# Two of four groups of both output projections token-stationary and turned through DRAM, another order for the third group, and the first down projection's sums turned off TensorE

## What is computed

```python
def short_conv_mixer(xn, w_in, conv_w, w_out):
    gb, gc, h = jnp.split(xn @ w_in, 3, axis=-1)
    return (gb * causal_dwconv(gc * h, conv_w)) @ w_out

def conv_glu_ffn(xn, w_up, conv_w, w_down):
    gate, val = jnp.split(causal_dwconv(xn @ w_up, conv_w), 2, axis=-1)
    return (jax.nn.silu(gate) * val) @ w_down

for i in range(2):
    xn = rms_norm(h, norm_mix[i])
    mix = hgrn2_mixer(xn, ...) if i == 0 else short_conv_mixer(xn, ...)
    h = h + mix
    h = h + conv_glu_ffn(rms_norm(h, norm_ffn[i]), w_up[i], conv_w[i], w_down[i])
return rms_norm(h, final_norm)
```

## Time and profile before

| | before |
|---|---|
| median of 3 runs | 2299.27 us (2299.03 to 2299.79) |
| the profiled execution | 2299.77 us, span 2297.9 us |
| TensorE / weight loads busy | 2285.5 us (99%) / 1916.0 us (83%) |
| VectorE / ScalarE busy | 1694.5 us (74%) / 1049.6 us (46%) |
| TensorE's granted clock, mean | 0.999 |
| `HGRN_OUT` on TensorE | 405.5 to 497.8 us |
| `DOWN0` | 977 to 1222.6 us |
| `SC_OUT` | 1482.6 to 1571.7 us |

### The profile page before, as it was taken

How to read it: one execution, slowest core, us unless ns; L and a number is a source line. 1 busy time by engine, 2 the same in 40 slices (tenths; PEclk the granted TensorE clock), 3 DMA queues, 4 the chain that set the end, 5 groups by cost and what they waited for, 6 DMA issues and landing times.

```text
span 2297.9 us, 33410 instructions
## 1 busy us (share of the span) xinstructions
PE 2285.5 (99%) x11110; PEld 1916.0 (83%) x11110; DVE 1694.5 (74%) x2132; ACT 1049.6 (46%) x1089; POOL 2.8 (0%) x9
## 2 busy tenths in 40 slices
PE   9999999999999999999999999999999999999998
PEld 8888888888888888888888888888888888888887
DVE  7979788877878888865556676766878878876544
ACT  7444444454444454444444333444444444444443
POOL 0000000000000000000000000000000000000000
PEclk9999999999999999999999999999999999999999
DMA  7555555558888888875667888666888888887664
GB/s 247 166 174 160 179 164 166 183 189 236 242 245 233 244 243 240 242 214 188 191 191 208 243 238 245 202 193 197 248 242 240 242 244 236 241 249 219 220 192 155
DMA packets 389733, 493.55 MB, mean 215 GB/s; under 512 B 18704, under 2 KB 223888, under 8 KB 389520
## 3 DMA queue, kind: packets, MB, share of 16 engines
q1 hardware_dynamic: 388640, 490.01, 71.9%
q10 hardware_dynamic: 1008, 2.43, 0.3%
HBM read 459.85 MB, written 30.41 MB: 213 GB/s over the span
## 4 chain that ended last, share of the span: by engine, by line
PE 89%; DVE 6%; issue 3%; DMA 1%; ACT 1%; DVEq 0%; SPq 0%; ACTq 0%
PE acc L1459 24%; PE acc L1458 24%; PE acc L1460 24%; PE acc L1392 11%; PE acc L1402 6%; DVE w_parts L742 1%; DVE a_diag L1062 1%; DVE fpre L1047 1%; DMA raw<-in_hgrn_w_in 1%; DVE kl L1029 1%; PE side L1563 0%; DVE ql L1023 0%; ACT w_parts L463 0%; DVE ta L778 0%; DVE ta L769 0%
## 5 line engine op out<-in xcount | busy, mean ns | idle before, releaser
L742 DVE TENSOR_TENSOR w_parts<-raw,w_parts 128x1024 fp32r<-128x1024 f32 x816 | 992.8, 1224 | 551.8 <-ACT w_parts L463 425.6
L463 ACT ACTIVATE w_parts<-raw 128x1024 fp32r<-128x1024 f32 x815 | 860.1, 1059 | 1061.0 <-PE acc L1460 827.7
L1458 PE MATMUL acc<-w_parts,xn 128*128 128x512 f32 x1728 | 673.3, 390 | 0.0
L1460 PE MATMUL acc<-w_parts,xn 128*128 128x512 f32 x1728 | 672.6, 389 | 0.0
L1459 PE MATMUL acc<-w_parts,xn 128*128 128x512 f32 x1728 | 672.6, 389 | 0.0
L1458 PEld LDWEIGHTS acc<-w_parts,xn 128*128 128x128 f32 x1728 | 324.4, 188 | 67.5
L1460 PEld LDWEIGHTS acc<-w_parts,xn 128*128 128x128 f32 x1728 | 324.4, 188 | 67.2
L1459 PEld LDWEIGHTS acc<-w_parts,xn 128*128 128x128 f32 x1728 | 324.4, 188 | 66.9
L1458 PE MATMUL acc<-w_parts,act 128*128 128x512 f32 x704 | 274.3, 390 | 0.0
L1460 PE MATMUL acc<-w_parts,act 128*128 128x512 f32 x704 | 274.0, 389 | 0.0
L1459 PE MATMUL acc<-w_parts,act 128*128 128x512 f32 x704 | 274.0, 389 | 0.0
(11 more groups left out here) (157 smaller groups left out, 1223.0 us busy)
## 6 DMA issues: line engine op xcount, KB each, us to landing
raw<-in_ffn_w_up SPq DMA_DIRECT2D x352, 512.0 KB, 4.4
raw<-in_ffn_w_down SPq DMA_DIRECT2D x176, 512.0 KB, 4.6
raw<-in_hgrn_w_in SPq DMA_DIRECT2D x127, 512.0 KB, 3.8
raw<-in_sc_w_in SPq DMA_DIRECT2D x96, 512.0 KB, 4.6
crossing<-turned SPq DMA_DIRECT2D x54, 512.0 KB, 3.8
moved<-crossing SPq DMA_DIRECT2D x216, 128.0 KB, 4.5
raw<-in_hgrn_w_out SPq DMA_DIRECT2D x32, 512.0 KB, 4.0
raw<-in_sc_w_out SPq DMA_DIRECT2D x32, 512.0 KB, 4.7
```

What stands on the lines that cost most here:

```text
L463: nc.scalar.activation(w_parts[:, c % RING, :, 0, :], raw[:, c % RING], ACT.Copy).then_inc(hi_ready, 1)
L742: v.tensor_tensor(w_parts[:, c % RING, :, 1, :], raw[:, c % RING], w_parts[:, c % RING, :, 0, :].bitcast(F32), ALU.subtract).then_inc(lo_r ...
L1458: mm(bank, x_hi, hi, start=begin and q == 0, stop=False)
L1460: high = mm(bank, x_lo, hi, start=False, stop=end and q == KC - 1)
```

## The change

`HGRN_OUT` and `SC_OUT` become phases of one iteration with two groups, token-stationary; new phases `HGRN_LAST` and `SC_OUT_LAST` hold groups three and four, feature-stationary as before. In the first two groups VectorE turns the sums at the last step, SyncE stores and fetches them, and VectorE adds them to `h` at step 4 of the next group (`ADDED_AT`; HGRN scales them first), ScalarE does its `residual` at step 5 and VectorE `normed` at step 6 (`behind`). The third group's order of chunks is new: part 0 at 0, 1, 2, 6 and part 1 at 3, 4, 5, 7; all its positions are in runs of two. For the first three groups of `DOWN0` VectorE's transposes (into `turned_sums`, in the memory of `pad`) and the way through DRAM (to `moved_sums`, in that of `tb`) take the place of ScalarE's copies and TensorE's turning; the fourth group keeps them.

```diff
-        elif first and g == 0 and self is HGRN_OUT:
-            order = [(0, 0), (0, 1), (1, 0), (1, 1), (0, 2), (1, 2), (0, 3), (1, 3)]
+        elif first and g == 0 and (self is HGRN_LAST or self is SC_OUT_LAST):
+            order = [(0, 0), (0, 1), (0, 2), (1, 0), (1, 1), (1, 2), (0, 3), (1, 3)]
         elif first and g == 0 and self is HGRN_IN:
             order = [(0, 0), (1, 0), (0, 1), (1, 1), (0, 2), (0, 3), (1, 2), (1, 3)]
...
-        paired = 0 if single else self.cpg - RUN if self is HGRN_OUT and first and g == 0 else end
+        paired = 0 if single else end
         return [range(k, k + RUN) for k in range(0, paired, RUN)] + [range(k, k + 1) for k in range(paired, end)]
...
 PAIR_SPLIT, OWN_PRODUCT, OWN_HIGH, OWN_LOW = 1, 9, 10, 12
 HGRN_IN = Phase(None, 4, 4, DT, scales=3, wide_group=V_GROUP)
-HGRN_OUT = Phase(HGRN_IN, 2, 2, DT)
-UP0 = Phase(HGRN_OUT, 11, 2, DT, scales=2, corrects=False, parts=1)
+HGRN_OUT = Phase(HGRN_IN, 1, 2, DT, scales=2, corrects=False, parts=1)
+HGRN_LAST = Phase(HGRN_OUT, 1, 2, DT)
+UP0 = Phase(HGRN_LAST, 11, 2, DT, scales=2, corrects=False, parts=1)
 DOWN0 = Phase(UP0, 2, 2, FT, corrects=False, parts=1)
 SC_IN = Phase(DOWN0, 1, 10, DT, scales=10, corrects=False, parts=1)
 SC_LAST = Phase(SC_IN, 1, 2, DT, scales=2)
-SC_OUT = Phase(SC_LAST, 2, 2, DT, corrects=False)
-UP1 = Phase(SC_OUT, 11, 2, DT, scales=2, corrects=False, parts=1)
+SC_OUT = Phase(SC_LAST, 1, 2, DT, corrects=False, parts=1)
+SC_OUT_LAST = Phase(SC_OUT, 1, 2, DT, corrects=False)
+UP1 = Phase(SC_OUT_LAST, 11, 2, DT, scales=2, corrects=False, parts=1)
 DOWN1 = Phase(UP1, 2, 2, FT, corrects=False, parts=1)
 CHUNKS = DOWN1.c0 + DOWN1.n * DOWN1.cpi
 
...
+ADDED_AT, SQUARED_AT, NORMED_AT = 4, 5, 6
 SCALED_AT, CONV_AT, PRODUCT_AT, SPLIT_HIGH_AT, SPLIT_LOW_AT = 5, 6, 9, 10, 11
 
...
 
-        turned_groups = {UP0: 0, SC_IN: UP0.n * UP0.groups, UP1: UP0.n * UP0.groups + SC_IN.groups}
+        turned_groups, groups = {}, 0
+        for phase in (HGRN_OUT, UP0, DOWN0, SC_IN, SC_OUT, UP1):
+            turned_groups[phase] = groups
+            groups += phase.n * phase.groups - (phase is DOWN0)
+        stored_groups = {phase: n - (DT // TG - 1) * (n > turned_groups[DOWN0]) for phase, n in turned_groups.items()}
+
+        turned_sums = pad[:, :, TAPS - 1:].rearrange("p q (b n) -> p q b n", b=T // P)
+        moved_sums = tb[:].rearrange("p j t -> p (j t)").rearrange("p (b a n) -> p b a n", b=T // P, a=4)
 
         block = ctx.enter_context(nc.Block())
 
...
+
+            def fetch(to):
+
                 for q in range(4):
-                    sp.dma_start(moved[q * QUARTER:(q + 1) * QUARTER].rearrange("f b a n -> f (b a) n"),
+                    sp.dma_start(to[q * QUARTER:(q + 1) * QUARTER].rearrange("f b a n -> f (b a) n"),
                                  crossing[q].rearrange("b (a f) n -> f (b a) n", f=QUARTER)).then_inc(moved_in, 16)
+
+            def cross_sums(n, kk):
+
+                if n and kk == STORED_AT:
+                    sp.wait_ge(turned_ready, turned_groups[DOWN0] + n)
+                    for b in range(T // P):
+                        sp.dma_start(crossing[:, b].rearrange("q p n -> p q n"), turned_sums[:, :, b]) \
+                            .then_inc(sums_stored, 16)
+                if n and kk == FETCHED_AT:
+                    sp.wait_ge(sums_stored, 16 * (T // P) * n)
+                    fetch(moved_sums)
 
             def cross(i, first, g, kk, up):
...
 
-            def cross_conv(g, kk):
-
-                if kk == STORED_AT and 0 < g <= SC_IN.groups:
-                    store_turned(0, SC_IN, g - 1)
-                if kk == FETCHED_AT - SC_IN.cpg and g > 1:
-                    fetch_moved(0, SC_IN, g - 2)
+            def cross_next(phase, g, kk):
+
+                if kk == STORED_AT and 0 < g <= phase.groups:
+                    store_turned(0, phase, g - 1)
+                if kk == FETCHED_AT - phase.cpg and 1 < g <= phase.groups + 1:
+                    fetch_moved(0, phase, g - 2)
+
+            def cross_down(i, first, g, kk):
+
+                if first:
+                    cross_last(UP0.n - 1, g * DOWN0.cpg + kk, UP0)
+                cross_sums(i * DOWN0.groups + g, kk)
 
             def stream(phase, w, column, ahead=None):
...
-            def residual_phase(phase, r0, weight, rs_n=None, carry=None):
+            def residual_phase(phase, last, r0, weight, rs_n=None, carry=None):
+
+                def behind(g, step):
+                    if g >= 0 and step == SQUARED_AT:
+                        for part in range(TG // TW):
+                            residual(0, r0 + g * (TG // TW), part, g * TG, weight)
+
                 def pieces(i, first, g, kk):
-                    if carry and first:
+                    if carry:
                         carry(g, kk)
-                    if rs_n is not None and first and (g, kk) == (0, RS_AT):
+                    if rs_n is not None and (g, kk) == (0, RS_AT):
                         root(rs_n)
-                    part, _, _, ends = phase.steps(first, g)[kk]
-                    tile = i * (2 * TG) + g * TG
-                    if rs_n is not None and kk == phase.cpg - 1:
-                        for part in range(phase.parts):
-                            residual(i, r0 + g * phase.parts, part, tile, weight)
...
+                if (n, kk) != (DT // TG - 1, DOWN0.cpg - 1):
                     return
                 act_e.wait_ge(lo_used, DOWN0.c0 + (n + 1) * DOWN0.cpg + RING)
-                if n:
-                    act_e.wait_ge(stage_done, S_DOWN + n)
                 for b in range(T // P):
                     o = nc.scalar.activation(sums[:, b], acc[:, (DOWN0.a0 + n) % SETS, b, :], ACT.Copy)
                 o.then_inc(acc_free, 1)
...
@@ -831,47 +876,83 @@
                 low_parts(tile + part * TW, weight, TW)
                 add_squares(i, 4, sq + part, sq + part, ta[:, part * TW:(part + 1) * TW, :])
 
-            def residual_phase(phase, r0, sq0, weight, rs_n=None, rs_stage=None, ahead=None):
+            def add_moved(phase, g, tile, src):
+
+                dve.wait_ge(moved_in, (turned_groups[phase] + g + 1) * 4 * 16)
+                dst = h[:, tile:tile + TG, :].rearrange("p j (s t) -> p s j t", t=QUARTER)
+                v.tensor_tensor(dst, dst, src.rearrange("p b a (j t) -> p (b a) j t", j=TG), ALU.add).then_inc(h_ready, 2)
+
+            def residual_phase(phase, last, r0, sq0, weight, rs_n=None, rs_stage=None, ahead=None):
                 carry = carried.pop() if carried else None
 
+                def behind(g, step):
+                    if g < 0:
+                        return
+                    tile, r, sq = g * TG, r0 + g * (TG // TW), sq0 + g * (TG // TW)
+                    if step == ADDED_AT and rs_n is not None:
+                        u = pad[:, :, TAPS - 1:]
+                        scaled_moved(0, phase, g, u)
+                        await_scaled(0, phase, g)
+                        for part in range(TG // TW):
+                            dst = h[:, tile + part * TW:tile + (part + 1) * TW, :]
+                            v.tensor_tensor(dst, dst, u[:, part * TW:(part + 1) * TW, :], ALU.add).then_inc(h_ready, 1)
+                    elif step == ADDED_AT:
+                        add_moved(phase, g, tile, moved[:])
+                    if step == NORMED_AT:
+                        dve.wait_ge(h_ready, r + TG // TW)
+                        for part in range(TG // TW):
+                            normed(0, phase, r, sq, part, tile, weight)
+
+                def turns(i, first, g, kk):
+                    if ahead:
+                        ahead(i, first, g, kk)
+                    if kk == phase.cpg - 1:
+                        turn_group(i, phase, g, turned[:])
+
                 def pieces(i, first, g, kk):
-                    if carry and first:
+                    if carry and not g:
                         carry(g, kk)
-                    if rs_n is not None and first and (g, kk) == (0, FOLD_OUT_AT):
+                    if rs_n is not None and (g, kk) == (0, FOLD_OUT_AT):
                         fold_squares(rs_n)
-                    if rs_n is not None and first and (g, kk) == (0, RS_AT):
+                    if rs_n is not None and (g, kk) == (0, RS_AT):
                         rms(rs_n, rs_stage)
-                    part, _, _, ends = phase.steps(first, g)[kk]
-                    tile = i * (2 * TG) + g * TG
-                    r, sq = (n0 + g * phase.parts for n0 in (r0, sq0))
-                    if rs_n is not None and kk == phase.cpg - 1:
-                        await_corrected(i, phase, g)
+                    behind(g - 1, kk)
+
+                def last_pieces(i, first, g, kk):
+                    if g == 0:
+                        behind(phase.groups - 1, kk)
+                    part, _, _, ends = last.steps(first, g)[kk]
+                    tile = (phase.groups + g) * TG
```

(55 more changed lines are left out.)

64 lines of the change are left out of this document (40 added, 24 removed).

## The result

The changed kernel takes 2308.2 us at the median (2307.5 to 2310.3, six runs) against 2299.2 before (2299.0 to 2299.8): ratio 1.0039, 95% interval 1.0030 to 1.0049, 9.0 us slower. The forecast was 2302.4, range 2299.8 to 2306.0. The profiled execution took 2307.5 us, the fastest of the six, its span 2305.6 (before 2297.9).

A forecast was written before the change was run, and what follows sets the result against it. TensorE, busy for 99% of the span, was taken to bound the kernel. Terms -2.0 - 2.7 + 2.5 + 5.3 = +3.1 us moved the median from 2299.27 to 2302.4; range 2299.8 to 2306.0.

The forecast's parts named there:

- part 3: Seven more groups' transfers through DRAM: cost nothing, fetched sums needed 13.6 us after the transposes, there after 11.2, 2.4 cover.
- the clock: Rival, chance 0.28: TensorE's clock falls to half in the 5.3 us stall only, costing 0 to 2.1 us; 2304.5.
- Part 1: Output projections: 32 chunks go token-stationary, 2.72 us each instead of 2.78, taking 2.0 us off.
- Part 2: First down projection: three of four turn stages on TensorE go, 0.89 us each, taking 2.7 us off.
- Part 4: Between third and fourth group, TensorE waits for position 6's acc set: 2.5 us in HGRN, 5.3 in short convolution.
- The rival of the late transfer: Chance 0.08: the DRAM detour lands 2 us after its cover in both output projections, stalls 4.5 and 7.3; 2306.4.
- No new stall: Rival, chance 0.12: TensorE doesn't wait between third and fourth group, leaving -4.7 us; 2294.6.
- shorter stalls: Rival, chance 0.10: ScalarE's squares don't delay VectorE's split of position 6, stalls 1.1 and 4.7 us; 2300.4.

The follow-up runs named there:

- the part alone: Kernel before, with only the first down projection's first three groups turned by VectorE and sent through DRAM: 2296.4 us, ratio 0.9986.
- parts one after the other: Changed kernel, third group of both output projections with part 0 at positions 0 to 3, part 1 at 4 to 7: 2297.8 us, ratio 0.9995.
- the runs of one: Changed kernel, last two positions of the third group run singly (highs 6, lows 6, highs 7, lows 7): 2307.3 us, ratio 1.0036.
- the moved steps: Kernel with parts one after the other, third group's scaling, adds, squares and norm steps moved to position 1 of the fourth: 2294.3 us, ratio 0.9978.
- the part-filled second wait: Changed kernel, 8 and 18 extra matmuls of ones ahead of TensorE's two waits before the fourth group: 2306.5 us, ratio 1.0028.
- the load first: Changed kernel, SyncE issuing the fourth group's position 1 weight load ahead of the second group's fetch: 2310.5 us, ratio 1.0045.
- the release first: Changed kernel, VectorE in the short convolution's third group releasing the acc set before the second group's norm steps: 2305.0 us, ratio 1.0024.

## Why the prediction was wrong

The two waits stand where the prediction put them and end on the instructions that it named, and the form and the down projection gave what it said. Two of its terms stood at nothing and weren't: the transfers (part 3) and the clock. The sum had the right sign (+3.1), but two thirds of the size were missing: of these 5.9 us the low clock is 3.5 and the late transfers are 1.9, which leaves 0.5 open. By its steps:

- **Part 1, form, -2.0:** right (2.1 between two kernels).
- **Part 2, down projection, -2.7:** right (3.1 for the part alone, which 2.7 agrees with within the interval).
- **Part 3, the detour "a cost of nothing, with 2.4 us of cover":** wrong, the smaller of the two terms that failed, 0.7 + 1.2 = 1.9 us of wait. I took the landing times of the page, medians over the whole kernel, 3.8 and 4.5 us for store and fetch, and gave the loads behind them no term at all. Here are the issues of the stretch itself (KB each, median us to landing):

```profile
raw<-in_hgrn_w_out SPq DMA_DIRECT2D x4, 512.0 KB, 7.5
...
moved<-crossing SPq DMA_DIRECT2D x4, 128.0 KB, 5.8
```

VectorE stands for 4 us in norm steps and transposes at the second group's end and then makes three splits in a row. SyncE's queue waits 3.6 us for the transposes, and then the store, four loads and the four fetches go out between 456.97 and 465: a load needs 7.5 us at the median, a fetch 5.8, and the last fetch, on which VectorE waits, some 7.6. So the sums are there 13.6 us after the transposes began and not 11.2, and the cover of 2.4 us is used up. The trace of before had a sign of it: in the nine microseconds around the detour of the earlier trace rows four loads took 6.2 us and the fetches 5.0. Why the loads were slower still here isn't shown. Both ends of it are on the chain: VectorE waits for the fetched sums, and ScalarE's split of position 5 waits for its weights and holds up the squares behind it:

```profile
1545.23 1.06 ACT L498 ACTIVATE w_parts<-raw 128x1024 fp32r<-128x1024 f32 x1 [3.39 <-DMA raw<-in_sc_w_out]
1546.20 0.90 ACT L549 ACTIVATE xn<-h,par 128x256 fp32r<-128x256 f32 x2
...
1548.84 1.04 ACT L498 ACTIVATE w_parts<-raw 128x1024 fp32r<-128x1024 f32 x1
```

- **Part 4, the waits of 2.5 and 5.3:** the chain right, its times late by that term. With 0 at the start of the run of positions 4 and 5 (1537.69 in the short convolution's projection): split at 4.88 (forecast 4.9), add at 6.4 (6.0), squares from 8.5 (7.2), VectorE's split of position 6 at 12.2 (11.0), norm steps done at 16.1 (15.0), set released at 17.6 (16.4). So 6.5 against 5.3. HGRN in the same way, 14.3 against 13.6, 3.2 against 2.5. The rival of the late transfer was this, at a price of 0.7 and 1.2 us and not 2 each. One comparison of part 4 was with the wrong group: part 0's end at position 5, and the last two positions as runs of their own, belong to the first group of a projection in the kernel before. Its third group had the parts one after the other, part 0 done at position 3.
- **The clock:** its rival was rated at 0.28, put in one wait and not in the other, and left out of the sum. It happened in both and cost 1.7 and 1.8 us, inside the bounds of 0 to 2.1. This is the larger term that failed, 3.5 us put at nothing. For the second wait the forecast went against its own reading: 5.3 us is past the 4.2 that I had read, and all that I had against the fall was that one fall fixes no distance. For the first wait the step that failed is the point from which it decides: I took the 4.2 us of the one fall in the trace as the least. In the runs here it fell from 2.2 to 5.3 us after the last matmul (the last section has them), so that a wait of 2.5 us was in question too, and a wait of that length with the runs of one had the fall. The rule of the Trainium skill (TensorE: Matmul & The Clock Gate, What's actually happening), that throttling is the default and activity lifts it, agrees with the way back: about 3.4 and 3.7 us of matmuls ran at 0.50 before 1.00 returned.
- **The forecast was a case without the rivals, and both came together.** Added up, -4.7 + 9.7 + 3.5 = +8.5, which is past the end of the range by 2 us. The range reached about as far as each rival alone and not as far as both. That the clock fell in the first wait only because late transfers had made it longer isn't shown: 2.5 us were enough elsewhere.
- **No new stall** and **shorter stalls** didn't happen. That ScalarE stands in the chain is shown by VectorE's idle time of 2.2 and 2.4 us ahead of its split of position 6, which ends on ScalarE's.

## What to carry to other kernels

When a kernel's bounding engine has no idle time, a part that ends late in one group and whose buffer is wanted at the start of the next is paid in full, so count the queue of the engine that releases it, let the part end earlier, and move steps that nobody waits for into the next group: here the order took off 10.4 us and the moved steps 3.5, which turned 9.0 us of loss into 5.2 of gain. Take transfer times from the stretch in which the transfer will run, not from the kernel's median; in a burst of loads behind a busy VectorE a fetch took a third longer than that median. A wait of 2.5 us and more on TensorE cost more than itself, 1.5 to 2.9 us here, and rivals that can come true together need a case of the forecast in which they do.

## What the runs showed of the hardware

- There is no fixed distance from TensorE's stop to the fall of the clock. From the last matmul to the change from 1.00 to 0.50 were 3.0 and 3.2 us in the changed kernel, 2.3 and 3.2 with the runs of one, 2.2 in the part-filled second wait, 3.8 and 4.3 with the load first, 5.3 and 4.0 with the release first, 4.2 at the end of before. In the case of 5.3 TensorE had been at work again for 0.8 us when it fell:

```profile
478.00:479.00 1.00, 0.39 (x2) 0.35 (x3) 1.00 (x3) 0.47 (x2) 0.00 (x0) 1.00 0.00 0
479.00:480.00 1.00, 1.00 (x5) 0.82 (x4) 1.00 (x3) 0.24 (x1) 0.00 (x0) 0.70 0.73 222
480.00:481.00 1.00, 1.00 (x4) 0.81 (x3) 1.00 (x3) 0.00 (x0) 0.00 (x0) 0.50 0.84 291
```

  By the starts of TensorE's instructions, it didn't fall in waits of 2.1 us (parts one after the other) and less, and each of the nine waits of 2.5 us and more had a fall. While TensorE worked on matmuls of ones, whose results nobody read, the clock stayed at 1.00.
- Behind the nine waits with a fall, 16 matmuls of 512 columns took 5.1 to 6.5 us instead of 3.65 (5.3 and 5.5 in the changed kernel, 6.5 in the part-filled wait); the clock was back at 1.00 before they ended.
- A fetch of 128 KB among several weight loads landed after 5.8 us at the median, the last of four after some 7.6, where the median of the kernel is 4.5, and the loads of 512 KB around it after 7.5.
